# Neighbourhood attention: VectorE takes each lane's maximum right behind its bias, and reciprocals of sums beside the normalising

## The chip, the cores and the metric

The kernel runs on one core of a Trainium2 chip. The time is the device time of one execution in microseconds (us), given as the median of several runs. The core's engines work side by side, each through its own instructions in order: TensorE (PE in the profile), VectorE (DVE), ScalarE (ACT), GpSimd (POOL) and SyncE (SP, which issues the DMAs). They wait for each other by semaphores only.

## The reference, cut to what matters

The program computes a two-layer network with an RWKV mix and a differential attention, and after it a block with two attentions over 512 tokens and a context of 256. The change lies in these two. Each has 8 heads of width 64 for the values. For a head, with 512 + 256 = 768 keys:

```python
# mla: block_attention
sc = einsum('bqhd,bkhd->bhqk', qblk, k) * scale
p = softmax(sc, axis=-1)
o = einsum('bhqk,bkhd->bqhd', p, v)
# na: neighborhood_attention, over a grid of 8 rows by 64 columns
s_win = einsum('bwhd,brwchd->bwhrc', qr, k_win) * scale + bias
s_ctx = einsum('bwhd,blhd->bwhl', qr, kc) * scale
p = softmax(concatenate([s_win, s_ctx], axis=-1), axis=-1)
o = p_win @ v_win + p_ctx @ vc
```

Only the neighbourhood attention adds a bias to its 512 window scores. In the kernel the bias table holds a large negative number outside the window of 16 columns, so all 512 are computed.

## The kernel before, in words

Nearly all of the program is dense layers: pairs of `weights_hi` and `weights_lo` made by ScalarE and VectorE, multiplied on TensorE (line 830). They follow each other with the mixing stages between them, and at the end of every stage each engine waits for the others (`fence`). The two attentions are stages of their own: `attention("mla", ...)` after the layer `uq`, and `attention("na", ...)` after the layers `kb`, `vb` and `qb`.

An attention works on four heads at once. Each has a **lane**, numbered 0 to 3: two PSUM banks (`flat`, 768 scores for 128 queries), a buffer for the probabilities, one for the turned probabilities, and four small columns `attn_small` (maximum, scaled maximum, sum, reciprocal). A head has `TB` = 4 blocks `tb` of 128 queries, each with 5 steps, and `woven` (line 88) writes the order down: step by step, all four lanes at a step before the next. So there are 2 x 4 **rounds**, and in a round every engine goes through its part of steps 0 to 4, lanes 0, 1, 2, 3 at each:

- step 0: TensorE computes the scores (lines 1305 and 1306). It waits for the lane's previous normalising. In `na` VectorE adds the bias (line 2454).
- step 1: VectorE takes the maximum over the 768 scores (line 2462), waits for it, and multiplies it by minus the scale (line 2464). ScalarE computes the exponential with this as its bias, and the sum along with it (line 1777).
- step 2: TensorE transposes the probabilities in six pieces (line 1311). VectorE takes the reciprocal of the sum (line 2468).
- step 3: the turned probabilities are copied out of PSUM, by VectorE in even blocks (line 2471), by ScalarE in odd ones (line 1781).
- step 4: TensorE multiplies by the values (line 1317). VectorE scales the result by the reciprocal (line 2475), which is the normalising.

This one list, `ATTN_ORDER`, sets the order of TensorE, ScalarE and VectorE in both attentions. The plan (`attention_plan`) counts the semaphore values in the same order: each lane has one semaphore for each engine.

The bias tables stand beside it. SyncE loads one for each head (line 2700) into the lane's buffer; for heads 4 to 7 it first waits for the lane's last addition of the head before, lane after lane, and GpSimd adds the window mask to the table (line 2602). VectorE's first addition of a head waits for the mask. Behind these loads SyncE's queue has the next weights.

## Time and profile before

| | us |
|---|---|
| median of 3 runs | 3412.47 |
| lowest and highest of them | 3405.42, 3415.96 |
| the profiled execution's own time | 3388.53 |
| its span, first to last instruction | 3386.7 |
| the mla attention in it, from 2797 to 2911 | 114 |
| the na attention in it, from 3000 to 3137 | 137 |

Times inside the trace are microseconds from the start of the span, and durations in the lists are microseconds unless marked ns. A stretch's clock is the one granted to TensorE, as a share of full speed: 1.00 is 2.4 GHz and 0.50 is 1.2 GHz. In a list in order of time, instructions of one line that follow each other are merged ("x24"), and the brackets give the idle time ahead of them and who ended it.

### The profile page before, as it was taken

The page shows a single profiled execution, that of the slowest core. Times are in us where ns is not written, and L with a number is a line of the kernel's source. Part 1 is how long each engine was busy: PE and PEld are TensorE (multiplying, and loading weights), DVE is VectorE, ACT ScalarE, POOL GpSimd, SP SyncE. Part 2 cuts the span into 40 slices and gives each one's busy share as a digit, 9 for nine tenths or more (in the row PEclk, how much of TensorE's full clock was granted, in tenths as well). Part 3 has the DMA queues.
Part 4 walks back from the last instruction along what each step waited for, and adds up shares of the span by engine and source line. Part 5 has one row for each costly group of instructions (what it writes and reads, how often), then busy time and mean ns, then how long its engine had stood idle before and what let it go on. Part 6 is the DMA issues. An engine that isn't in the chain of part 4 may idle for free.

```text
span 3386.7 us, 39065 instructions
## 1 busy us (share of the span) xinstructions
PE 3149.7 (93%) x15716; PEld 2508.4 (74%) x15716; DVE 1666.8 (49%) x2751; ACT 1149.6 (34%) x1853; POOL 142.1 (4%) x145
## 2 busy tenths in 40 slices
PE   7999889899998889999999999769999989988998
PEld 6888567666667768888788888548888767877886
DVE  5434543456655654344754345775535435245235
ACT  4222133344444333223332224453323333233332
POOL 0000000211211100000000000000000000000000
PEclk9999999799999999999999999779999989987999
DMA  4333232000000033333233332003333110201231
GB/s 127 97 96 94 63 111 75 27 28 28 28 28 15 1 118 100 99 94 100 75 100 94 99 97 88 1 22 101 96 94 95 61 38 1 85 13 47 85 96 56
DMA packets 173896, 234.77 MB, mean 69 GB/s; under 512 B 14201, under 2 KB 111062, under 8 KB 173462
## 3 DMA queue, kind: packets, MB, share of 16 engines
q1 hardware_dynamic: 173718, 232.29, 22.1%
q8 instruction: 125, 2.05, 0.3%
q14 instruction: 53, 0.43, 0.0%
HBM read 228.05 MB, written 4.19 MB: 69 GB/s over the span
## 4 chain that ended last, share of the span: by engine, by line
PE 84%; DVE 9%; ACT 4%; issue 2%; POOL 1%; DMA 0%; SPq 0%; DVEq 0%; ACTq 0%
PE banks L830 63%; PE banks L1317 3%; PE banks L972 2%; PE banks L1311 1%; PE banks L963 1%; PE banks L1305 1%; PE banks L1007 1%; PE banks L1034 1%; PE banks L940 1%; PE banks L1030 1%; PE banks L981 1%; DVE diff_scores L2316 1%; DVE diff_small L2322 1%; PE banks L918 1%; ACT L1556 1%
## 5 line engine op out<-in xcount | busy, mean ns | idle before, releaser
L1865 DVE TENSOR_TENSOR weights_lo<-weights_raw,weights_hi 128x1024 fp32r<-128x1024 f32 (+2 forms) x393 | 472.8, 1206 | 1038.2 <-ACT weights_hi L1388 1036.9
L830 PE MATMUL banks<-operand_hi,weights_hi 128*128 128x512 f32 x2208 | 873.0, 395 | 28.3 <-DVE weights_lo L1865 14.5
L830 PE MATMUL banks<-operand_lo,weights_hi 128*128 128x512 f32 x2208 | 865.9, 392 | 0.0
L830 PE MATMUL banks<-operand_hi,weights_lo 128*128 128x512 f32 x2208 | 865.6, 392 | 0.0
L1388 ACT ACTIVATE weights_hi<-weights_raw 128x1024 fp32r<-128x1024 f32 (+2 forms) x393 | 407.9, 1041 | 1090.9 <-PE banks L830 1049.5
L830 PEld LDWEIGHTS banks<-operand_hi,weights_hi 128*128 128x128 f32 x2208 | 418.4, 189 | 123.2 <-issue 25.8
L830 PEld LDWEIGHTS banks<-operand_lo,weights_hi 128*128 128x128 f32 x2208 | 418.9, 190 | 88.6 <-issue 2.2
L830 PEld LDWEIGHTS banks<-operand_hi,weights_lo 128*128 128x128 f32 x2208 | 418.3, 189 | 88.3
L972 PE MATMUL banks<-operand_lo 128*128 128x512 f32 x370 | 173.2, 492 | 1.3 <-ACT v L1508 1.3
L830 PE MATMUL banks<-hidden_ffn_hi,weights_hi 128*128 128x512 f32 x352 | 137.1, 390 | 0.0
L830 PE MATMUL banks<-hidden_ffn_hi,weights_lo 128*128 128x512 f32 x352 | 136.9, 389 | 0.0
L830 PE MATMUL banks<-hidden_ffn_lo,weights_hi 128*128 128x512 f32 x352 | 136.9, 389 | 0.0
L830 PE MATMUL banks<-hidden_ffn_mid_hi,weights_hi 128*128 128x512 f32 x352 | 136.9, 389 | 0.0
L830 PE MATMUL banks<-hidden_ffn_mid_lo,weights_hi 128*128 128x512 f32 x352 | 136.9, 389 | 0.0
L830 PE MATMUL banks<-hidden_ffn_mid_hi,weights_lo 128*128 128x512 f32 x352 | 136.9, 389 | 0.0
L972 PEld LDWEIGHTS banks<-operand_lo 128*128 128x128 f32 x370 | 70.0, 200 | 27.8 <-issue 22.9
L830 PEld LDWEIGHTS banks<-hidden_ffn_hi,weights_hi 128*128 128x128 f32 x352 | 66.1, 188 | 13.8
L830 PEld LDWEIGHTS banks<-hidden_ffn_mid_hi,weights_hi 128*128 128x128 f32 x352 | 66.1, 188 | 13.8
L830 PEld LDWEIGHTS banks<-hidden_ffn_hi,weights_lo 128*128 128x128 f32 x352 | 66.1, 188 | 13.8
L830 PEld LDWEIGHTS banks<-hidden_ffn_mid_lo,weights_hi 128*128 128x128 f32 x352 | 66.1, 188 | 13.7
L830 PEld LDWEIGHTS banks<-hidden_ffn_mid_hi,weights_lo 128*128 128x128 f32 x352 | 66.1, 188 | 13.7
L830 PEld LDWEIGHTS banks<-hidden_ffn_lo,weights_hi 128*128 128x128 f32 x352 | 66.1, 188 | 13.6
(509 smaller groups left out, 4424.7 us busy)
## 6 DMA issues: line engine op xcount, KB each, us to landing
weights_raw<-in_ffn_w_in_dram SPq DMA_DIRECT2D x352, 256.0 KB, 3.0
weights_raw<-in_ffn_w_out_dram SPq DMA_DIRECT2D x88, 512.0 KB, 3.7
weights_raw<-in_w_in_dram SPq DMA_DIRECT2D x36, 512.0 KB, 3.6
weights_raw<-in_rwkv_w_rkv_dram SPq DMA_DIRECT2D x24, 512.0 KB, 3.8
weights_raw<-in_w_mod_dram SPq DMA_DIRECT2D x24, 512.0 KB, 4.9
weights_raw<-in_w_kv_dram SPq DMA_DIRECT2D x16, 512.0 KB, 3.6
weights_raw<-in_rwkv_w_o_dram SPq DMA_DIRECT2D x8, 512.0 KB, 5.3
weights_raw<-in_diff_w_q_dram SPq DMA_DIRECT2D x8, 512.0 KB, 4.3
```

Of the source, the lines that this page charges most:

```text
L830: mm = nc.tensor.matmul(o, l, r, start=first and t == 0 and job["opens"], stop=last and t == 2, **skip)
L918: mm = nc.tensor.matmul(ps[p0:p0 + c1 - c0, job["bank"]], ring_raw[:, u["ring"], kk, c0:c1], mixed[:, k % 4], start=k == 0, stop=k == KC - 1)
L940: mm = nc.tensor.matmul(ps[0:2, MISC_BANK], sc[:, k], ring_raw[:, units[uid]["ring"], k % 2, :], start=k == 0, stop=k == KC - 1)
L963: mm = nc.tensor.matmul(ps[:, b, tb * 256:(tb + 1) * 256], lhs[h0:h0 + HEAD, tb * P:(tb + 1) * P], L.ar[h0:h0 + HEAD, tb, :, :], start=Tru ...
L972: nc.tensor.matmul(ps[:, IDLE_BANK], two_ident, two_ident.unsqueeze(1).broadcast_to([P, 4, P]), start=True, stop=True)
L981: mm = nc.tensor.matmul(ps[:, b], ring_raw[p0:p0 + n, u["ring"], 0, 0:P], rhs[p0:p0 + n, :], start=j == 0, stop=j == len(ids) - 1)
L1007: mm = nc.tensor.matmul(ps[:, b, p * P:(p + 1) * P], L.mh[:, p], L.inv[:, p], start=True, stop=True)
L1030: mm = nc.tensor.matmul(ps[:, b, p * P:(p + 1) * P], L.xm[:, p], L.inv_t[:, p], start=True, stop=True)
L1034: mm = nc.tensor.matmul(ps[:, b, p * P:(p + 1) * P], L.inv_t[:, p], L.xm[:, p], start=True, stop=True)
L1317: mm = nc.tensor.matmul(ps[:, A, 0:MLA_V], turned_[:, lane, kt * P:(kt + 1) * P], value(hd, kt), start=kt == 0, stop=kt == KEY_TILES - 1)
L1388: nc.scalar.activation(ring_hi[0:p, u["slot"], 0:n, 0:w], ring_raw[0:p, u["ring"], 0:n, 0:w], ACT.Copy).then_inc(*weights_hi.by(i))
L1865: nc.vector.tensor_tensor(ring_lo[0:p, u["slot"], 0:n, 0:w], ring_raw[0:p, u["ring"], 0:n, 0:w], f32(ring_hi[0:p, u["slot"], 0:n, 0:w]), A ...
```

## The change

`ATTN_ORDER` becomes a table with one order for each attention; both are still the same list. VectorE's code changes in two ways. In `na` the maximum and its scaling move from step 1 to step 0, right behind the lane's bias addition, for which the maximum waits. In both attentions the reciprocals move from step 2 to step 4, each ahead of its lane's normalising. The new function `row_maximum` holds the two instructions that `mla` still has in step 1. No instruction is added or taken away.

```diff
--- before.py
+++ after.py
@@ -538,10 +538,10 @@
         operand_plan("cq", 2)
         add_dense("uq", "act", n=4)
         close("uq")
-        ATTN_ORDER = woven(MLA_HEADS, 5 * TB, LANES, False)
+        ATTN_ORDER = {"mla": woven(MLA_HEADS, 5 * TB, LANES, False), "na": woven(NA_HEADS, 5 * TB, LANES, False)}
 
         def attention_plan(name):
-            for hd, lane, s in ATTN_ORDER:
+            for hd, lane, s in ATTN_ORDER[name]:
                 tb, s = divmod(s, 5)
                 if s == 0:
                     lane_pe[lane].expect((name, "s", hd, tb))
@@ -551,15 +551,14 @@
                     lane_dve[lane].expect((name, "max", hd, tb))
                     lane_act[lane].expect((name, "exp", hd, tb))
                 elif s == 2:
-                    lane_dve[lane].expect((name, "rs", hd, tb))
                     lane_pe[lane].expect((name, "turn", hd, tb))
                 elif s == 3:
                     (lane_act if tb % 2 else lane_dve)[lane].expect((name, "turned", hd, tb))
                 else:
                     lane_pe[lane].expect((name, "o", hd, tb))
+                    lane_dve[lane].expect((name, "rs", hd, tb))
                     lane_dve[lane].expect((name, "o", hd, tb))
 
-        attn_lane = {hd: lane for hd, lane, s in ATTN_ORDER}
         attention_plan("mla")
         close("mla")
 
@@ -1292,7 +1291,7 @@
 
             def attention(name, scores, value, prev_ready):
                 probs_, turned_ = probs[name]
-                for hd, lane, s in ATTN_ORDER:
+                for hd, lane, s in ATTN_ORDER[name]:
                     A, B = 2 * lane, 2 * lane + 1
                     flat = ps[:, A:B + 1].rearrange("p a b -> p (a b)")
                     tb, s = divmod(s, 5)
@@ -1768,7 +1767,7 @@
 
             def attention(name, scale):
                 probs_, turned_ = probs[name]
-                for hd, lane, s in ATTN_ORDER:
+                for hd, lane, s in ATTN_ORDER[name]:
                     A, sm = 2 * lane, attn_small[:, lane]
                     flat = ps[:, A:A + 2].rearrange("p a b -> p (a b)")
                     tb, s = divmod(s, 5)
@@ -2440,13 +2439,21 @@
                     dve.wait_ge(*q_sin.at(hd))
                     nc.vector.tensor_tensor(qa[:, hd], qa[:, hd], s, ALU.add).then_inc(*q_done.by(hd))
 
+            def row_maximum(name, hd, lane, tb, scale):
+                sm, flat = attn_small[:, lane], ps[:, 2 * lane:2 * lane + 2].rearrange("p a b -> p (a b)")
+                nc.vector.tensor_reduce(sm[:, 0:1], flat[:, 0:KEYS], AX_X, ALU.max).then_inc(*dve_own.by())
+                dve.wait_ge(*dve_own.now())
+                nc.vector.tensor_scalar(sm[:, 1:2], sm[:, 0:1], -scale, None,
+                                        ALU.mult).then_inc(*lane_dve[lane].by((name, "max", hd, tb)))
+
             def attention(name, o_all, scale):
                 turned_ = probs[name][1]
-                for hd, lane, s in ATTN_ORDER:
+                for hd, lane, s in ATTN_ORDER[name]:
                     A, B, sm, own = 2 * lane, 2 * lane + 1, attn_small[:, lane], lane_dve[lane]
                     flat = ps[:, A:B + 1].rearrange("p a b -> p (a b)")
                     tb, s = divmod(s, 5)
                     if s == 0 and name == "na":
+
                         e0 = NA_KR - 2 - 2 * tb
                         dve.wait_ge(*lane_pe[lane].at((name, "s", hd, tb)))
                         if tb == 0:
@@ -2454,22 +2461,17 @@
                         nc.vector.tensor_tensor(ps[:, A], ps[:, A],
                                                 bias[:, lane, e0:e0 + NA_KR, :].rearrange("p e c -> p (e c)"),
                                                 ALU.add).then_inc(*own.by((name, "bias", hd, tb)))
-                    elif s == 1:
-                        if name == "na":
-                            dve.wait_ge(*own.at((name, "bias", hd, tb)))
-                        else:
-                            dve.wait_ge(*lane_pe[lane].at((name, "s", hd, tb)))
-                        nc.vector.tensor_reduce(sm[:, 0:1], flat[:, 0:KEYS], AX_X, ALU.max).then_inc(*dve_own.by())
-                        dve.wait_ge(*dve_own.now())
-                        nc.vector.tensor_scalar(sm[:, 1:2], sm[:, 0:1], -scale, None,
-                                                ALU.mult).then_inc(*own.by((name, "max", hd, tb)))
-                    elif s == 2:
-                        dve.wait_ge(*lane_act[lane].at((name, "exp", hd, tb)))
-                        nc.vector.reciprocal(sm[:, 3:4], sm[:, 2:3]).then_inc(*own.by((name, "rs", hd, tb)))
+                        dve.wait_ge(*own.at((name, "bias", hd, tb)))
+                        row_maximum(name, hd, lane, tb, scale)
+                    elif s == 1 and name != "na":
+                        dve.wait_ge(*lane_pe[lane].at((name, "s", hd, tb)))
+                        row_maximum(name, hd, lane, tb, scale)
                     elif s == 3 and tb % 2 == 0:
                         dve.wait_ge(*lane_pe[lane].at((name, "turn", hd, tb)))
                         nc.vector.tensor_copy(turned_[:, lane], flat[:, 0:KEYS]).then_inc(*own.by((name, "turned", hd, tb)))
                     elif s == 4:
+                        dve.wait_ge(*lane_act[lane].at((name, "exp", hd, tb)))
+                        nc.vector.reciprocal(sm[:, 3:4], sm[:, 2:3]).then_inc(*own.by((name, "rs", hd, tb)))
                         dve.wait_ge(*lane_pe[lane].at((name, "o", hd, tb)))
                         dve.wait_ge(*own.at((name, "rs", hd, tb)))
                         nc.vector.tensor_scalar(o_all[:, tb, hd * MLA_V:(hd + 1) * MLA_V], ps[:, A, 0:MLA_V], sm[:, 3:4],
```

VectorE's rows around one round of `na`, an even block of the first four heads. `banks` are the scores in PSUM, `lane0_pe` is TensorE's semaphore for lane 0, and so on. Before, steps 0 and 1:

```order
L2454 TENSOR_TENSOR banks<-banks,window_bias 128x512 [waits lane0_pe]
L2454 TENSOR_TENSOR banks<-banks,window_bias 128x512 [waits lane1_pe]
L2454 TENSOR_TENSOR banks<-banks,window_bias 128x512 [waits lane2_pe]
L2454 TENSOR_TENSOR banks<-banks,window_bias 128x512 [waits lane3_pe]
L2462 TENSOR_REDUCE attn_small<-banks 128x1 [waits lane0_dve]
L2464 TENSOR_SCALAR attn_small<-attn_small 128x1 [waits dve_own]
L2462 TENSOR_REDUCE attn_small<-banks 128x1 [waits lane1_dve]
L2464 TENSOR_SCALAR attn_small<-attn_small 128x1 [waits dve_own]
L2462 TENSOR_REDUCE attn_small<-banks 128x1 [waits lane2_dve]
L2464 TENSOR_SCALAR attn_small<-attn_small 128x1 [waits dve_own]
L2462 TENSOR_REDUCE attn_small<-banks 128x1 [waits lane3_dve]
L2464 TENSOR_SCALAR attn_small<-attn_small 128x1 [waits dve_own]
```

Now, the same places:

```order
L2461 TENSOR_TENSOR banks<-banks,window_bias 128x512 [waits lane0_pe]
L2444 TENSOR_REDUCE attn_small<-banks 128x1 [waits lane0_dve]
L2446 TENSOR_SCALAR attn_small<-attn_small 128x1 [waits dve_own]
L2461 TENSOR_TENSOR banks<-banks,window_bias 128x512 [waits lane1_pe]
L2444 TENSOR_REDUCE attn_small<-banks 128x1 [waits lane1_dve]
L2446 TENSOR_SCALAR attn_small<-attn_small 128x1 [waits dve_own]
L2461 TENSOR_TENSOR banks<-banks,window_bias 128x512 [waits lane2_pe]
L2444 TENSOR_REDUCE attn_small<-banks 128x1 [waits lane2_dve]
L2446 TENSOR_SCALAR attn_small<-attn_small 128x1 [waits dve_own]
L2461 TENSOR_TENSOR banks<-banks,window_bias 128x512 [waits lane3_pe]
L2444 TENSOR_REDUCE attn_small<-banks 128x1 [waits lane3_dve]
L2446 TENSOR_SCALAR attn_small<-attn_small 128x1 [waits dve_own]
```

The second lane's addition stood second, ahead of all maxima; now it stands behind the first lane's maximum and scaling.

The rows that follow them in the same round, steps 2 to 4. Before (`na_probs_turned` is the copy of step 3, `na_out` the normalised result):

```order
L2468 RECIPROCAL attn_small<-attn_small 128x1 [waits lane0_act]
L2468 RECIPROCAL attn_small<-attn_small 128x1 [waits lane1_act]
L2468 RECIPROCAL attn_small<-attn_small 128x1 [waits lane2_act]
L2468 RECIPROCAL attn_small<-attn_small 128x1 [waits lane3_act]
L2471 COPY na_probs_turned<-banks 128x768 [waits lane0_pe]
L2471 COPY na_probs_turned<-banks 128x768 [waits lane1_pe]
L2471 COPY na_probs_turned<-banks 128x768 [waits lane2_pe]
L2471 COPY na_probs_turned<-banks 128x768 [waits lane3_pe]
L2475 TENSOR_SCALAR na_out<-banks,attn_small 128x64 [waits lane0_dve,lane0_pe]
L2475 TENSOR_SCALAR na_out<-banks,attn_small 128x64 [waits lane1_dve,lane1_pe]
L2475 TENSOR_SCALAR na_out<-banks,attn_small 128x64 [waits lane2_dve,lane2_pe]
L2475 TENSOR_SCALAR na_out<-banks,attn_small 128x64 [waits lane3_dve,lane3_pe]
```

Now:

```order
L2471 COPY na_probs_turned<-banks 128x768 [waits lane0_pe]
L2471 COPY na_probs_turned<-banks 128x768 [waits lane1_pe]
L2471 COPY na_probs_turned<-banks 128x768 [waits lane2_pe]
L2471 COPY na_probs_turned<-banks 128x768 [waits lane3_pe]
L2474 RECIPROCAL attn_small<-attn_small 128x1 [waits lane0_act]
L2477 TENSOR_SCALAR na_out<-banks,attn_small 128x64 [waits lane0_dve,lane0_pe]
L2474 RECIPROCAL attn_small<-attn_small 128x1 [waits lane1_act]
L2477 TENSOR_SCALAR na_out<-banks,attn_small 128x64 [waits lane1_dve,lane1_pe]
L2474 RECIPROCAL attn_small<-attn_small 128x1 [waits lane2_act]
L2477 TENSOR_SCALAR na_out<-banks,attn_small 128x64 [waits lane2_dve,lane2_pe]
L2474 RECIPROCAL attn_small<-attn_small 128x1 [waits lane3_act]
L2477 TENSOR_SCALAR na_out<-banks,attn_small 128x64 [waits lane3_dve,lane3_pe]
```

The four reciprocals stood between the last scaling and the first copy. Now nothing stands there, and each reciprocal is directly ahead of its lane's normalising. In `mla` the reciprocals move in the same way, and in odd blocks there are no copies on VectorE.

## Rows read from the trace of the kernel before

**Rows 1.** The page, parts 1 and 2: busy us, share, instructions; slices

```profile
PE 3149.7 (93%) x15716; PEld 2508.4 (74%) x15716; DVE 1666.8 (49%) x2751; ACT 1149.6 (34%) x1853; POOL 142.1 (4%) x145
...
PEclk9999999799999999999999999779999989987999
```

**Rows 2.** Stage table: length, PE, PEld, DVE, ACT, POOL busy, clock, DMA; mla, then na

```profile
2797.00:2911.00 114.00, 110.41 (x704) 88.83 (x704) 60.88 (x144) 44.03 (x81) 0.00 (x0) 0.98 0.00 1
3000.00:3137.00 137.00, 109.81 (x704) 100.00 (x704) 78.53 (x175) 43.56 (x81) 8.24 (x4) 0.80 0.10 29
```

**Rows 3.** Waits of the na stage (3000 to 3138): total, times, longest us

```profile
PE banks L1311 <- ACT na_probs L1777: 27.0, 8, 3.5
```

**Rows 4.** Chain of waits, one na round: start us, us, what

```profile
3034.72 1.06 PE banks L1305 x4
3035.78 0.43 PE banks L1306 x3
...
3036.24 2.59 DVE banks L2454 x4
3038.83 0.86 DVE attn_small L2462
...
3039.72 0.17 DVE attn_small L2464
...
3039.90 1.00 ACT na_probs L1777 x2
...
3040.95 5.38 PE banks L1311 x24
3046.33 5.47 PE banks L1317 x48
```

**Rows 5.** Stage table by stretches of this round, columns as in rows 2

```profile
3040.00:3046.00 6.00, 5.05 (x24) 5.05 (x25) 5.03 (x13) 3.87 (x8) 0.00 (x0) 0.50 0.00 1
3046.00:3047.00 1.00, 1.00 (x9) 1.00 (x7) 1.00 (x2) 0.00 (x0) 0.00 (x0) 0.72 0.07 16
3047.00:3052.00 5.00, 5.00 (x46) 4.93 (x46) 1.71 (x5) 0.00 (x0) 0.00 (x0) 1.00 0.00 0
```

**Rows 6.** TensorE in order of time, this round: start us, us, instructions, idle before

```profile
3036.90 0.70 PE L1306 MATMUL banks<-na_keys,na_queries 64*128 64x256 f32 x4
3040.95 5.38 PE L1311 MATMUL banks<-ident,na_probs 128*128 128x128 f32 x24 [3.35 <-ACT na_probs L1777]
```

**Rows 7.** TensorE in order of time, mla stage, an even block

```profile
2859.85 2.13 PE L1311 MATMUL banks<-ident,mla_probs 128*128 128x128 f32 x18
```

**Rows 8.** VectorE in order of time, the same na round

```profile
3038.74 0.95 DVE L2462 TENSOR_REDUCE attn_small<-banks 128x1 f32<-128x768 f32 x1
...
3039.79 0.95 DVE L2462 TENSOR_REDUCE attn_small<-banks 128x1 f32<-128x768 f32 x1
...
3042.87 0.15 DVE L2464 TENSOR_SCALAR attn_small<-attn_small 128x1 f32<-128x1 f32 x1
...
3049.16 0.28 DVE L2475 TENSOR_SCALAR na_out<-banks,attn_small 128x64 f32<-128x64 f32 x1 [1.06 <-PE banks L1317]
```

**Rows 9.** ScalarE in order of time, na, an odd block: copies of the turned

```profile
3061.04 2.20 ACT L1781 ACTIVATE na_probs_turned<-banks 128x768 f32<-128x768 f32 x3
```

**Rows 10.** One line and one tile: count, min/median/max ns: additions, reciprocals

```profile
L2454 DVE TENSOR_TENSOR banks<-banks,window_bias x32: 689/690/700, 3002.0 to 3123.5; 128x512 f32<-128x512 f32 x32
...
L2468 DVE RECIPROCAL attn_small<-attn_small x64: 142/149/166, 2805.4 to 3129.5; 128x1 f32<-128x1 f32 x64
```

**Rows 11.** Chain of waits, mla stage, an even block

```profile
2862.25 0.17 DVE attn_small L2468
2862.42 0.86 DVE mla_probs_turned L2471
```

**Rows 12.** Waits of the mla stage (2797 to 2911)

```profile
PE banks L1317 <- DVE mla_probs_turned L2471: 0.7, 4, 0.2
```

**Rows 13.** GpSimd in order of time, na stage: the masks of the later heads

```profile
3061.06 6.16 POOL L2602 TENSOR_TENSOR window_bias<-window_bias,window_mask 128x896 f32<-128x896 f32 x3 [0.46 <-DMA window_bias<-in_rpb_dram]
```

## The prediction

> **What bounds the kernel now.** I read the page first: TensorE is busy 93% of the span, VectorE 49%, and TensorE's clock falls from full in only a few slices [rows 1]. So a change on VectorE counts only where TensorE stands waiting for it. The change touches two stages, and the stage table shows how different they are. The latent attention ("mla", 114 us) keeps TensorE busy for 110.41 us at a granted clock of 0.98. The neighbourhood attention ("na", 137 us) has it busy for 109.81 us at a clock of 0.80 [rows 2]. The waits of the second stage say for what: TensorE waits 27.0 us, in 8 waits, for ScalarE's exponential [rows 3]; the chain below leads on to VectorE. There are 8 because the stage has 8 rounds (2 groups of 4 heads by 4 query blocks).
>
> The chain of waits through one round tells what VectorE has on the path [rows 4]: scores 1.49 us, all four bias additions 2.59, one maximum 0.86 and its scaling 0.17, one exponential 1.00, then TensorE's 24 transposes 5.38 and the 48 passes with the values 5.47. With the gaps that is 17.1 us, and 8 rounds are the stage. The other three maxima are not on the path. They run beside the transposes. The granted clock of this round is 0.50 from 3040 to 3046 and 1.00 from 3047 [rows 5]. That is 1.2 GHz for the transposes, after TensorE stood idle for 3.35 us [rows 6]. One transpose costs 5.38/24 = 0.224 us there, and 2.13/18 = 0.118 us in the mla stage at full clock [rows 6, 7].
>
> **The order of VectorE in na.** Before, in the round at 3036.24: four additions, then four pairs of maximum and scaling. The first scaling starts at 3039.72, the fourth at 3042.87, so they follow each other at 1.05 us; ScalarE starts lane 0's exponential 0.18 us after its scaling, at 3039.90 [rows 4, 8]. Now the maximum waits for the addition just issued. An addition takes 0.70 us (689 to 700 ns, [rows 10]) while four of them in a row took 2.59 [rows 4], so (2.59 - 0.69)/3 = 0.63 us each when nothing waits. The price of a dependent pair I take from maximum to scaling, 3038.74 to 3039.72: 0.98 us from start to start for an instruction of 0.95 [rows 4, 8], so 0.03 behind the end. So lane 0's maximum starts at 3036.24 + 0.73 = 3036.97, its scaling 0.98 later at 3037.95, that is **1.77 us earlier**. Each next lane needs 0.73 + 0.98 + 0.07 (3039.72 to 3039.79, scaling to the next start [rows 4, 8]) = 1.78 us instead of 1.05: scalings at 3039.73, 3041.51, 3043.29. Lane 3 is **0.42 us later** than before. The exponentials follow, and TensorE can transpose lane 3 from 3043.29 + 0.18 + 1.05 = 3044.52 (1.05: exponential start 3039.90 to transpose start 3040.95 [rows 4]).
>
> **What TensorE makes of it.** It starts lane 0 at 3040.95 - 1.77 = 3039.18. At 1.2 GHz a lane's six transposes take 1.35 us, so it is through with lane 2 before lane 3 is ready, stands about 0.4 us between lanes, and ends at 3044.52 + 1.35 = 3045.87 instead of 3046.33 (3040.95 + 5.38). The gain is 0.46 us a round, not 1.77: what is late next is the last lane's maximum. The value passes can follow at once, in even blocks because VectorE copies lane 0 from 3043.36, in odd ones because ScalarE does from about 3044.5 at 0.73 each (2.20/3, [rows 9]). But the clock rose only behind the transposes: the microsecond from 3046 is at 0.72, so 0.56 of it was low and the rise came at 3046.56 [rows 5]. If it stays there, 0.46 us more of value passes run at 1.2 GHz and 0.22 us of the gain goes back (0.46 x (1 - 0.118/0.224), the passes taken as slowing like the transposes). That leaves 0.24 us a round, 8 x 0.24 = **1.9 us**. Bounds for this term: 8 x 0.46 = 3.7 us if the rise comes earlier by as much; a loss if it comes later (second rival).
>
> The self-wait was priced at 0.73 - 0.63 = 0.10 us a lane, 0.4 us a round. The additions show what a missing wait is worth: they follow each other at 0.63 us though each lasts 0.69. The Trainium skill ("VectorE: DVE Perf Modes", The DRAIN you can't avoid) reports eight copies that took the same time with and without a semaphore behind each, and takes such a semaphore to cost nothing. By that rule the last lane would be level with before, each round about 0.4 us shorter, and the sum some 3 us better. The trace's additions don't agree with it, so I keep my price.
>
> **The reciprocals.** 64 of them, 142 to 166 ns [rows 10], move behind the copies and stand before the normalising of their lane. In the mla stage the one of lane 3 holds back lane 0's copy in even blocks: 0.17 us in the chain, then the copy 0.86, and TensorE waits 0.18 us for it; 4 waits, 0.7 us [rows 11, 12]. Without it the copy starts right behind the last scaling, beside lane 3's exponential of 1.00 us, and is done before TensorE needs it: **0.7 us** saved. In na the transposes hide it. In the new place they are free: VectorE idles 1.06 us before each normalising [rows 8], the sum is long there, and the next scores wait only for lane 0's normalising, three lanes earlier. The cover holds as long as a lane's passes (5.47/4 = 1.37 us) exceed 0.28 + 0.15.
>
> **What moves with it.** SyncE reloads a lane's bias table only after that lane's last addition. In round 4 these now come at steps of 1.78 us instead of 0.63, the last 3 x 1.15 = 3.4 us later. GpSimd's last mask then ends near 3067.2 + 3.4 = 3070.6 [rows 13]; VectorE's addition for that lane comes in round 5, two rounds after this one, at 3036.24 + 2 x 17.1 + 3 x 1.78 = 3075.8. Hidden, with 5 us to spare; so are the weight loads behind it in SyncE's queue, needed after the stage's end at 3137. TensorE's and ScalarE's own orders are unchanged.
>
> **Sum.** 1.9 + 0.7 = 2.6 us: 3388.53 of the profiled execution becomes 3385.9. That execution lies 0.7% below the median of the three timed runs, 3412.47, which themselves spread over 10.5 us. I set the sum against the median: **3410 us**, 0.08% less. What a measurement of this kernel can tell from no change is about 0.3%, 10 us; the gain is far under it.
>
> **Rivals.** (1) *The clock no longer falls.* TensorE now idles only from 3037.6 (3036.90 + 0.70, [rows 6]) to 3039.18, 1.6 us instead of 3.35, and mla's shorter waits left its clock at 0.98. Then lane 3 ends at 3044.52 + 0.71 = 3045.23, 1.10 us a round: 8.8 + 0.7 = 9.5 us, 3403. Against it: until 3044.5 TensorE would work 0.71 us in each 1.78. (2) *The clock rises later: slower.* It rose 5.6 us after TensorE had begun to work without a gap (3040.95 to 3046.56). Now the work is unbroken only from 3044.52. If the rise follows that start as before, it comes at 3050.1, and 4.2 us of value passes run at 1.2 GHz where 0.2 did: 4.0 x 0.47 = 1.9 us back, 1.9 - 0.46 = +1.4 a round, some +11.5 in 8, less 0.7 is 3423. The gain of 0.46 is used up when 1.0 us more of the passes is low, that is by a rise at about 3047.1. I hold it second, because at the low clock TensorE would still be busy for 1.35 of each 1.78 us, and only the last gap of 0.4 lies near the rise. The Trainium skill ("TensorE: Matmul & The Clock Gate", A second HAM failure mode) describes a kernel in which short idle stretches between groups of matmuls kept the clock going down and up. By that rule this rival comes first and the time is 3423; no stretch of this trace shows such gaps inside a burst of transposes. (3) *The order is neutral*: the rise moves so that each round takes 17.1 us as before, since VectorE's work in a round is the same; with mla's 0.7 that is 3412. The rows of the changed order leave no doubt that it does what it says.
>
> **How the numbers follow.** Forecast (within a few us of 3410) 0.60; first rival 0.06; second 0.26, of which about half lies beyond the 10 us; neutral 0.08. Range: from the first rival, 3402, to the second, 3424. Faster by over 0.3%: 0.06, the first rival with a little help; slower: 0.15; within: 0.79.
>
> **What would show it.** Right: in na, additions and maxima alternate, scalings 1.78 us apart; TensorE's first wait near 1.6 us and three of about 0.4; clock 0.50 through the transposes; rounds of 16.8 to 17.1 us; mla rounds of even blocks 0.18 shorter. Wrong: value passes for microseconds at 0.50 (rounds over 17.5 us), or no fall of the clock (rounds of 16.0).

## The result and the profile after

The changed kernel takes 3410.79 us (median of 20 runs, 3403.64 to 3440.4), the kernel before 3397.97 us in as many (3382.91 to 3421.27). The ratio is **1.0042**, 95% interval 1.0021 to 1.0062: slower by 0.4%. The forecast was 3410 us, 0.08% less, too little to tell from no change. Its 3410 us lies beside the measured median only because the three runs of before that it started from, 3412.47 us, stood above the median that more runs gave. That is luck. The ratio is what counts, and it went the other way.

The profiled executions are 3388.53 us before and 3407.91 us now. The difference is 19.4 us. One place is 20.9 us longer, the na stage (136.7 us from its first to its last matmul before, 157.6 now); mla gave back 1.6.

The stage table of the changed kernel, mla and na, columns as in [rows 2]:

```profile
2797.00:2910.00 113.00, 109.53 (x704) 88.78 (x704) 61.25 (x145) 44.08 (x81) 0.00 (x0) 0.98 0.00 1
3001.00:3159.00 158.00, 128.29 (x704) 107.84 (x704) 81.25 (x176) 42.95 (x80) 8.24 (x4) 0.75 0.09 26
```

In mla TensorE is busy for nearly the same time (109.53 us, before 110.41) at the same clock. In na its 704 matmuls are the same ones, but they cost 128.29 us instead of 109.81, at a granted clock of 0.75 instead of 0.80. So TensorE waited only 2.5 us longer (29.7 us not busy against 27.2); it worked more slowly. The waits of the na stage, beside [rows 3]:

```profile
ACT na_probs L1776 <- DVE attn_small L2446: 110.8, 32, 16.5
...
PE banks L1310 <- ACT na_probs L1776: 29.6, 32, 1.9
```

29.6 us in 32 waits, where it was 27.0 in 8: the one wait of 3.35 us in each round has become four short ones.

The chain of waits through na, all of its eight value passes (start us, us, what); one round before had 5.47 [rows 4]:

```profile
3013.08 10.13 PE banks L1316 x48
...
3035.30 5.40 PE banks L1316 x48
...
3052.09 10.13 PE banks L1316 x48
...
3074.90 5.42 PE banks L1316 x48
...
3091.77 10.13 PE banks L1316 x48
...
3113.99 5.40 PE banks L1316 x48
...
3130.78 10.13 PE banks L1316 x48
...
3153.50 5.40 PE banks L1316 x48
```

Here is the time. In the first, third, fifth and seventh round the passes take 10.13 us, in the others 5.40. Rounds are 22.1, 17.5, 21.5, 18.1, 21.6, 17.5, 21.5 and 17.8 us long, where all were about 17.1.

TensorE in order of time, the third round, beside [rows 6]:

```profile
3042.89 0.70 PE L1305 MATMUL banks<-na_keys,na_queries 64*128 64x256 f32 x4
3045.18 0.88 PE L1310 MATMUL banks<-ident,na_probs 128*128 128x128 f32 x6 [1.59 <-ACT na_probs L1776]
3046.97 0.87 PE L1310 MATMUL banks<-ident,na_probs 128*128 128x128 f32 x6 [0.91 <-ACT na_probs L1776]
3048.76 1.54 PE L1310 MATMUL banks<-ident,na_probs 128*128 128x128 f32 x6 [0.91 <-ACT na_probs L1776]
3050.55 1.54 PE L1310 MATMUL banks<-ident,na_probs 128*128 128x128 f32 x6 [0.25 <-ACT na_probs L1776]
3051.88 10.34 PE L1316 MATMUL banks<-na_values,na_probs_turned 128*128 128x64 f32 x48
3062.15 2.08 PE L1304 MATMUL banks<-na_keys,na_queries 64*128 64x512 f32 x4
```

The wait ahead of lane 0 is 1.59 us, and there is a gap ahead of every lane. Two lanes are transposed at full clock (0.87 us), then the clock falls and two take 1.54; the 48 passes of 64 columns follow without any gap for 10.34 us, and the next scores take 2.08 us instead of 1.14. By stretches, beside [rows 5]:

```profile
3044.00:3048.00 4.00, 1.75 (x12) 1.27 (x12) 3.86 (x8) 2.27 (x5) 0.00 (x0) 0.97 0.00 0
3048.00:3052.00 4.00, 3.00 (x14) 2.60 (x14) 3.93 (x6) 1.70 (x4) 0.00 (x0) 0.50 0.02 6
3052.00:3062.00 10.00, 10.00 (x49) 10.00 (x48) 2.15 (x9) 0.00 (x0) 0.00 (x0) 0.50 0.00 0
3062.00:3065.00 3.00, 3.00 (x12) 1.73 (x13) 0.28 (x1) 0.00 (x0) 0.00 (x0) 0.53 0.00 0
3065.00:3071.00 6.00, 3.15 (x21) 2.00 (x19) 5.76 (x10) 2.46 (x5) 0.96 (x1) 1.00 0.63 160
```

TensorE was busy for all of the 10 us from 3052 and stayed at 0.50, that is 1.2 GHz. It came back to 1.00 only within the next scores, which are 512 and 256 columns wide: the stretch from 3062 is at 0.53, that from 3065 at 1.00.

The fourth round begins its last two lanes with the same gaps, to 0.01 us, and also at the low clock:

```profile
3071.57 1.53 PE L1310 MATMUL banks<-ident,na_probs 128*128 128x128 f32 x6 [0.91 <-ACT na_probs L1776]
3073.36 1.54 PE L1310 MATMUL banks<-ident,na_probs 128*128 128x128 f32 x6 [0.26 <-ACT na_probs L1776]
```

Yet its passes take 5.42 us: the clock is 0.50 until 3075 and 0.99 in the microsecond behind it. So the gaps make a bad round possible, but they don't decide alone which round is bad.

VectorE in order of time, the same round, beside [rows 8]:

```profile
3042.22 0.70 DVE L2461 TENSOR_TENSOR banks<-banks,window_bias 128x512 f32<-128x512 f32 x1 [1.20 <-PE banks L1305]
3042.96 0.96 DVE L2444 TENSOR_REDUCE attn_small<-banks 128x1 f32<-128x768 f32 x1
3043.95 0.15 DVE L2446 TENSOR_SCALAR attn_small<-attn_small 128x1 f32<-128x1 f32 x1
3044.02 0.69 DVE L2461 TENSOR_TENSOR banks<-banks,window_bias 128x512 f32<-128x512 f32 x1
...
3045.74 0.15 DVE L2446 TENSOR_SCALAR attn_small<-attn_small 128x1 f32<-128x1 f32 x1
...
3049.31 0.15 DVE L2446 TENSOR_SCALAR attn_small<-attn_small 128x1 f32<-128x1 f32 x1
```

This is as forecast: scalings 1.78 to 1.79 us apart, the maximum 0.74 us behind the start of its addition (forecast 0.73).

### The profile page after: what moved, and what is told of

It reads as the page before. It is cut to its first block, busy times and chain, and to the rows that moved or that the text cites. A ratio compares the mean times of both kernels' runs of the same rounds, so it can differ in the third digit from the quotient of the medians.

```text
span 3406.1 us, 39065 instructions
## 1 busy us (share of the span) xinstructions
PE 3164.3 (93%) x15716; PEld 2514.8 (74%) x15716; DVE 1670.3 (49%) x2751; ACT 1149.2 (34%) x1853; POOL 141.6 (4%) x145
## 4 chain that ended last, share of the span: by engine, by line
PE 83%; DVE 10%; ACT 4%; issue 2%; POOL 1%; DMA 0%; SPq 0%; DVEq 0%; ACTq 0%
PE banks L829 63%; PE banks L1316 3%; PE banks L971 2%; PE banks L1304 1%; PE banks L962 1%; DVE attn_small L2444 1%; PE banks L1006 1%; PE banks L1033 1%; PE banks L939 1%; PE banks L1029 1%; PE banks L980 1%; DVE diff_scores L2315 1%; DVE diff_small L2321 1%; PE banks L917 1%; DVE banks L2461 1%
## 5 line engine op out<-in xcount | busy, mean ns | idle before, releaser
L829 PE MATMUL banks<-hidden_ffn_hi,weights_lo 128*128 128x512 f32 x352 | 136.9, 389 | 0.0
L829 PE MATMUL banks<-hidden_ffn_lo,weights_hi 128*128 128x512 f32 x352 | 136.9, 389 | 0.0
L829 PE MATMUL banks<-hidden_ffn_mid_hi,weights_hi 128*128 128x512 f32 x352 | 136.9, 389 | 0.0
L829 PE MATMUL banks<-hidden_ffn_mid_lo,weights_hi 128*128 128x512 f32 x352 | 136.9, 389 | 0.0
L829 PE MATMUL banks<-hidden_ffn_mid_hi,weights_lo 128*128 128x512 f32 x352 | 136.9, 389 | 0.0
L971 PEld LDWEIGHTS banks<-operand_lo 128*128 128x128 f32 x370 | 70.0, 200 | 27.8 <-issue 22.9
```

Of the source, the lines that this page charges most:

```text
L829: mm = nc.tensor.matmul(o, l, r, start=first and t == 0 and job["opens"], stop=last and t == 2, **skip)
L971: nc.tensor.matmul(ps[:, IDLE_BANK], two_ident, two_ident.unsqueeze(1).broadcast_to([P, 4, P]), start=True, stop=True)
```

## The experiments

Two theories stood against each other. **The clock**: the gaps between the lanes' transposes let it fall and keep it from rising behind them, and the narrow value passes cannot bring it back. **The order**: VectorE's new order costs the time itself, by its self-waits, by the later last lane, or by the reciprocals in front of the normalising. "na" is the stage from its first to its last matmul in the profiled execution of each kernel; 136.7 us before, 157.6 changed. Ratios are against the kernel before on the same chip. Each of them has its own group of runs, and a single profiled execution need not be the median one.

**One half at a time.** First the reciprocals alone, on the kernel before:

```diff
-                    elif s == 2:
-                        dve.wait_ge(*lane_act[lane].at((name, "exp", hd, tb)))
-                        nc.vector.reciprocal(sm[:, 3:4], sm[:, 2:3]).then_inc(*own.by((name, "rs", hd, tb)))
                     elif s == 4:
+                        dve.wait_ge(*lane_act[lane].at((name, "exp", hd, tb)))
+                        nc.vector.reciprocal(sm[:, 3:4], sm[:, 2:3]).then_inc(*own.by((name, "rs", hd, tb)))
                         dve.wait_ge(*lane_pe[lane].at((name, "o", hd, tb)))
```

> The kernel before with the reciprocals moved beside the normalising, in both attentions; the maxima stay where they were. Clock theory (the time went into TensorE's clock, because the maxima behind their biases tear gaps into the transposes): nothing of the loss is here. The na stage stays at 136.7 us with rounds of 17.1 us and the clock at 0.50 only for the transposes; mla shortens from 113.2 to 111.6 us as in the changed kernel; in all 1 to 2 us less than before, no change that can be measured. Rival (the reciprocal in front of each normalising holds up TensorE's next scores): na grows towards 157 us and the time by 10 us or more.

Measured: ratio 0.9987 (0.9957 to 1.0016), na 136.9 us, seven of the eight rounds between 16.9 and 17.2, mla 111.4 instead of 113.2. None of the loss is here.

Then the maxima alone: the changed kernel with the two reciprocal lines put back into step 2.

> The changed kernel with the reciprocals put back behind the exponentials: only the maxima are moved. Clock theory: the whole loss is here. The na stage takes about 157 us, with rounds of some 21.5 us in which the 48 value passes take 10.1 us at 1.2 GHz and rounds of 17.5 us between them; mla is at 113 us as before; the time is 0.4 to 0.6% over before. Rival (reciprocals): na at 137 us.

Measured: ratio 1.0052 (1.0021 to 1.0084), na 153.8 us, mla 113.2. The value passes on its chain of waits, in the order of the rounds:

```profile
3014.47 10.13 PE banks L1316 x48
...
3036.69 5.40 PE banks L1316 x48
...
3053.47 10.13 PE banks L1316 x48
...
3075.44 5.40 PE banks L1316 x48
...
3091.79 9.31 PE banks L1316 x48
```

The passes of the other three rounds take 5.40, 9.24 and 5.41 us, so four of eight are long again. The loss is in the maxima: 17.1 of the 20.9 us of the na stage in this execution, and a timed ratio no smaller than the changed kernel's.

The fifth round shows something more. All four lanes are transposed at full clock (0.87 to 0.88 us each, with gaps of 0.93 to 0.94 us between them), the passes begin at full clock, and it falls about 1.3 us into them: the microsecond from 3092 is at 1.00, that from 3093 at 0.56, and the rest at 0.50. So the transposes need not run slowly for the passes to.

**The order kept, the gaps closed.** The changed kernel, with one wait more on TensorE:

```diff
                     elif s == 2:
+                        if name == "na" and lane == 0:
+                            pe.wait_ge(*lane_act[1].at((name, "exp", hd + 1, tb)))
                         pe.wait_ge(*lane_act[lane].at((name, "exp", hd, tb)))
```

> The changed kernel with one wait more: in na TensorE starts lane 0's transposes only when lane 1's exponential is done too. VectorE's order is that of the changed kernel. Clock theory: at 1.2 GHz the transposes then run from 4.7 us behind the first bias addition without a gap (1.35 us for a lane, the lanes come at 1.78), the clock rises behind them as before, the value passes are at full clock, rounds are 17.1 us and na takes 137 to 138 us; the time is level with before. Rival (the loss is VectorE's order: self-waits, the last lane's maximum 0.42 us later, work held up on its queue): a wait added can give nothing back, na stays at 157 us or more.

Measured: ratio 0.9979 (0.9950 to 1.0009), na 136.9 us, rounds of 17.1. TensorE in order of time:

```profile
3039.16 5.38 PE L1312 MATMUL banks<-ident,na_probs 128*128 128x128 f32 x24 [3.39 <-ACT na_probs L1778]
3044.34 5.65 PE L1318 MATMUL banks<-na_values,na_probs_turned 128*128 128x64 f32 x48
```

24 transposes in one piece, 3.39 us of idle time ahead of them, the same 5.38 us as in [rows 6], and passes at 5.65. A wait **added** takes back the 20 us, with VectorE's order untouched. It does two things at once: it closes the gaps between the lanes, and it gathers the idle time in one stretch ahead of them. No run here does one without the other.

**The other way round: the old order, with gaps.** Into the kernel before go unread additions that space the maxima like the new order does, and the same wait on TensorE closes the gaps again in a second kernel:

```diff
                         nc.vector.tensor_scalar(sm[:, 1:2], sm[:, 0:1], -scale, None,
                                                 ALU.mult).then_inc(*own.by((name, "max", hd, tb)))
+                        if name == "na" and lane < LANES - 1:
+                            nc.vector.tensor_tensor(sq_sum[:, :], rstd[:, :], rstd[:, :], ALU.add)
```

> The kernel before, in its old order; only, behind the scalings of lanes 0, 1 and 2 in na VectorE makes one addition of 128x512 in SBUF that nobody reads (about 0.65 us), so that the scalings come at 1.7 us instead of 1.05 and the transposes get the gaps of the changed kernel. By VectorE's work alone lane 3 comes about 2.0 us later, its transposes end 1.2 us later and rounds take 18.3 us: na 146 us. Clock theory: in every second round or more the value passes run at 1.2 GHz as well (10.1 us), such rounds take about 23 us, and na is 160 us or more, although the order of the change is not there. Rival (the loss comes with the new order): 146 us.

> The kernel with the spaced maxima, and TensorE starts lane 0's transposes only when lane 1's exponential is done too. VectorE's work is the same, the gaps in the transposes are gone. Clock theory: value passes are at full clock in most rounds, which take 18.2 to 19 us; na is 146 to 152 us, less than without the wait. Rival: the same as without the wait, or more.

Measured: 1.0047 (1.0013 to 1.0081) with na 157.4 us, and 1.0002 (0.9971 to 1.0033) with na 154.5. The first is the loss in the old order, though under the 160 us expected: only two of eight rounds have long passes (10.13 and 10.15 us), not every second one, and one of the two is the round spoken of below. In the second one round of 25.6 us was left, against the expectation. VectorE in that round:

```profile
3059.34 0.68 DVE L2469 TENSOR_TENSOR squares_sum<-rstd 128x512 f32<-128x512 f32 x1
...
3060.99 2.57 DVE L2469 TENSOR_TENSOR squares_sum<-rstd 128x512 f32<-128x512 f32 x1
...
3064.54 1.51 DVE L2469 TENSOR_TENSOR squares_sum<-rstd 128x512 f32<-128x512 f32 x1
```

The addition in SBUF takes 0.68 us elsewhere, but 2.57 and 1.51 beside GpSimd's masks, which ran from 3060.94. The experiment had torn gaps of its own (TensorE waited 0.72 and 0.95 us inside the transposes). So the pair was repeated without the additions in that one round:

```diff
-                        if name == "na" and lane < LANES - 1:
+                        if name == "na" and lane < LANES - 1 and (hd >= LANES or tb < TB - 1):
```

> The kernel with the spaced maxima again, but without the unread additions in the one round in which GpSimd adds its masks (there they had taken up to 2.6 us beside GpSimd, and torn gaps of their own). By VectorE's work alone na takes 7 rounds of 18 and one of 17.1 us: 144 us. Clock theory: one round or more still has its value passes at 1.2 GHz (10.1 us), na over 150 us.

> The same with TensorE's wait for lane 1's exponential ahead of lane 0's transposes: no gaps in any round now. Clock theory: no round has its value passes at 1.2 GHz; rounds of 17.5 to 19 us, na 142 to 146 us, and less than without the wait. Rival (the first round of the other pair, in which the wait did not help, was not GpSimd's doing): a round of over 20 us again.

Measured: without the wait 1.0057 (1.0023 to 1.0092), na 160.3 us, three rounds of 22.5 to 22.9 and one of 20.4; with it 1.0019 (0.9987 to 1.0052), na **144.3** us, no round over 19.0. The order is the old one in both and VectorE's work is the same; closing the gaps is worth 16 us. The medians of the timed runs, on one chip, are as far apart: 3415.62 and 3399.42 us.

Over all these kernels the count is plain. In 40 rounds the clock fell and the transposes then ran in one piece (before, the reciprocals alone, the wait added to the changed kernel, and the spaced kernels where the gaps were closed or left out); their passes took at most 5.7 us in every one. In 40 rounds there were gaps between the lanes (changed, the maxima alone, the spaced ones, and the changed kernel with five unread matmuls a round below); in 16 of them the passes took 9.2 us or more, in the others at most 5.6.

**TensorE kept busy.** If its own idling makes the clock fall, unread matmuls should hold it up. They go into the quarter of lane 3's second bank that holds no scores, and lane 3's maximum waits for them:

```diff
                     elif s == 2:
+                        if name == "na" and lane in {0: 12}:
+                            spare = ps[:, 2 * LANES - 1, CTX:T]
+                            for _ in range({0: 12}[lane]):
+                                mm = nc.tensor.matmul(spare, ident[:, :], f32(op[0][:, 0, 0:T - CTX]), start=True, stop=True)
+                            if lane == 0:
+                                mm.then_inc(*filler.by((hd - lane, tb)))
                         pe.wait_ge(*lane_act[lane].at((name, "exp", hd, tb)))
```

> The kernel before; in na TensorE makes 12 matmuls of 128x256 that nobody reads while it waits for lane 0's exponential (into an unused quarter of lane 3's bank, and lane 3's maximum waits for them). Clock theory: TensorE is no longer idle for 3.35 us a round, so the clock stays at 1.00; transposes cost 0.12 us instead of 0.22, but lane 3's wait for its exponential (44.1 on the clock of the round shown) now ends last: rounds of about 15.8 us, na 126 to 128 us, the time 9 to 11 us (0.3%) under before. Rival (the granted clock has a cause other than TensorE's own idling here, or the filler lands on the path): na stays at 137 us or grows.

Measured: 0.9986 (0.9959 to 1.0012), na 136.1 us at a clock of 1.00. The clock part was right and the time (126 to 128 us expected) was not: the 12 took 5.45 us in a wait of 3.35, since each is two passes of 0.227, so the filler itself came onto the path. With 7 of them, and with the reciprocals moved or not:

> The kernel before with the reciprocals moved and 7 unread matmuls of 128x256 ahead of lane 0's transposes (3.2 us; with 12 they took 5.45 us and held up lane 3's maximum and the transposes). Clock theory: clock 1.00 through na, transposes 0.12 us each, lane 3's end 10.1 us behind the start of the scores, rounds 15.5 us, na 125 us instead of 136.9; mla 111.6 us; 12 to 14 us (0.4%) under before. If the filler still lands on the path, rounds stay over 16.5 us.

> The kernel before with the 7 unread matmuls alone, reciprocals where they were. Clock theory: as the kernel with the reciprocals moved, but lane 3's reciprocal holds up the first copy in even blocks now that the transposes no longer hide it: rounds of 15.9 us in even blocks and 15.5 in odd ones, na 126 us, mla 113 us; 10 us (0.3%) under before. Rival: no change from before.

Measured: with the reciprocals moved 0.9954 (0.9922 to 0.9985), na **125.0** us, rounds of 15.5 to 15.7; without, 0.9977 (0.9944 to 1.0009), which is not clear of no change, na 126.8 us, rounds of 16.0 and 15.7 in turn. TensorE in order of time, the first of these two:

```profile
3036.70 3.29 PE L1313 MATMUL banks<-operand_hi,ident 128*128 128x256 f32 x14
3040.12 0.87 PE L1318 MATMUL banks<-ident,na_probs 128*128 128x128 f32 x6
3041.17 0.88 PE L1318 MATMUL banks<-ident,na_probs 128*128 128x128 f32 x6 [0.18 <-ACT na_probs L1784]
...
3043.30 0.88 PE L1318 MATMUL banks<-ident,na_probs 128*128 128x128 f32 x6 [0.20 <-ACT na_probs L1784]
```

Six transposes take 0.87 us, and the waits of 0.2 us between lanes do no harm, since the clock is up and stays up. With the reciprocals moved this is the one kernel whose interval lies under 1. Its mla stage took 113.0 us and not the 111.6 expected: from 2799 to 2808 us, at its first scores, the clock was 0.59 in this execution.

The same on the changed kernel (`{0: 3, 1: 2}`, the last one signalling), where only two of the four gaps can be filled, since lane 3's maximum then reads the bank:

> The changed kernel; in na TensorE makes 3 matmuls of 128x256 that nobody reads ahead of lane 0's transposes and 2 ahead of lane 1's (0.45 us each, into the unused quarter of lane 3's bank, whose maximum waits for them). Its gaps ahead of lanes 2 and 3 stay. Clock theory: the clock stays at 1.00 or falls in few rounds; where it stays, lane 3's transposes end about 10.5 us behind the start of the scores and rounds take 15.9 us, na 128 us or, with some rounds low, up to 145; in no case 157. The cost of VectorE's order without the clock is then the difference to the next kernels: some 0.3 us a round. Rival (VectorE's order costs the 20 us): na stays at 157 us.

Measured: na 141.9 us; six rounds have passes of 5.3 to 5.4 us, two of 10.13. The rounds entirely at full clock take 16.1 us, against 15.6 to 15.7 with the old order: that 0.4 to 0.5 us a round, some 3.6 us in all, is what the order itself costs. The timed runs do not show this gain over the changed kernel: 1.0036 (1.0001 to 1.0070). Two gaps left open, of 0.91 to 0.93 us, are enough for the clock to fall in some rounds, and how many it is in the other executions stays open.

**Wide matmuls ahead of the narrow ones.** Why does the clock stay low through 10 us of unbroken work? The changed kernel with five wide unread matmuls right ahead of the value passes:

```diff
                         pe.wait_ge(*(lane_act if tb % 2 else lane_dve)[lane].at((name, "turned", hd, tb)))
+                        if name == "na" and lane == 0:
+                            for _ in range(5):
+                                nc.tensor.matmul(ps[:, B, CTX:T], ident[:, :], f32(op[0][:, 0, 0:T - CTX]), start=True, stop=True)
```

> The changed kernel; in na TensorE makes 5 unread matmuls of 128x256 right ahead of lane 0's value passes (2.3 us in all at 2.4 GHz, 4.3 at 1.2). In the changed kernel's bad rounds the 48 value passes of 64 columns follow each other for 10.1 us without a gap and the clock stays at 1.2 GHz until the next scores, which are 512 wide. If it is their narrowness that keeps it there, the wide ones bring the clock up within the round: no round has all passes at 1.2 GHz, the passes take 8 us or less in the bad rounds, and the next scores are at full clock. Rival (the clock comes back only so long after the gaps, whatever TensorE does): passes of 10.1 us at 1.2 GHz as before, na 157 us plus 8 x 2.3 to 4.3.

Measured: na 153.8 us, less than the changed kernel's 157.6 although 8 x 2.3 us of work at the least was added; over all runs 1.0081 (1.0046 to 1.0116). The chain of waits, two of the rounds whose transposes fell to 1.2 GHz, the wide ones (L1317) and the passes (L1319):

```profile
3012.99 4.03 PE banks L1317 x10
3017.02 5.30 PE banks L1319 x48
...
3051.98 3.32 PE banks L1317 x10
3055.30 5.30 PE banks L1319 x48
```

The passes of all eight rounds take 5.30 to 5.32 us. The wide matmuls begin at 1.2 GHz and take 4.03 or 3.32 us instead of 2.25, and behind them the clock is up. The expectation held in full in this execution. So the clock does not simply come back a fixed time after the gaps: in the changed kernel the passes at this place left it low. Whether it is the 64 columns of a pass or something else in which the two kinds of matmul differ was not tried. The kernel is no improvement in itself, since the wide ones cost about what they save.

## Why the prediction was wrong

**The loss came by the second rival** ("the clock rises later: slower"), which had 0.26. It had the kind of loss right, passes at 1.2 GHz behind a late rise. It was held second for a wrong reason, was sized at half, and its rule for the rise, 5.6 us after the last gap, held in none of the changed kernel's eight rounds.

**The step that failed** is "If it stays there", the assumption under *What TensorE makes of it* that the rise comes at the same place as before, just behind the transposes. The changed kernel's chain shows that in four of eight rounds it does not come there at all. The fall was misplaced too. The sum lets all 24 transposes run at 1.2 GHz (1.35 us a lane), as before. In no round of the changed kernel did they: in the second and sixth none fell to it, in the first three lanes, in the others about two. What spoke against the rival, TensorE busy for 1.35 of each 1.78 us at the low clock, was no reason: all three other kernels with such gaps (the maxima alone moved, and the two spaced ones) have rounds in which the passes run at the low clock, and with the gaps closed by a wait it rose, but for the one round in which VectorE's unread additions, beside GpSimd's masks, made new ones.

**The size.** The rival lets the rise come 5.6 us after the last gap, so that 4 us of passes run low: +1.4 us a round, 11.5 in all. Measured are 20.9. In the third round the rise came about 14 us after the last gap (3050.55), in the fourth, with the same gaps, 1.6 us after it (3073.36). The rival took it for granted that any unbroken work brings the clock up. The value passes don't: in a bad round all 48 are low (10.13 - 5.40 = 4.7 us more), and the first of the next scores with them (2.08 us against 1.14). Four rounds are 4.4 to 4.8 us longer than their counterparts before, 18.2 us; the other four, which begin with scores at the low clock, 0.4 to 1.0 us, 2.7 in all. These are no worse because behind the scores the clock is back at 1.00. In the second and sixth round it stays there, in the fourth and eighth it falls and returns as the passes begin. So bad and good rounds alternate, which the forecast, with eight equal rounds, did not see. Why the fourth and eighth get the clock back in time and the third and seventh don't stays open.

**VectorE's terms** were right, or nearly. Scalings come 1.78 us apart (sum: 1.78), lane 0's is 1.75 us earlier behind the first addition (sum: 1.77), and the fourth starts 7.09 us behind it, before 6.63: 0.46 later (sum: 0.42). The first wait was put at 1.6 us and is 1.59. The self-wait was priced at 0.10 us. The maximum starts 0.74 us behind its addition. In the kernel before a maximum whose own addition was long done starts 0.60 us behind the last addition (3038.74 in [rows 8], less 3036.24 + 2.59 - 0.69 in [rows 4]), so the wait costs 0.14 us a lane, and the price, taken from additions at 0.63 us, was a little low. So the rule of the Trainium skill ("VectorE: DVE Perf Modes", The DRAIN you can't avoid), by which the semaphore costs nothing, does not hold for this pair, and the round at full clock with its 0.4 to 0.5 us says the same.

**The reciprocals** were right in sign and small in size: 0.7 us forecast, 1.6 measured in mla (113.2 to 111.6), and 1.8 with the reciprocals alone. The chain of waits there, changed kernel, beside [rows 11]:

```profile
2862.34 0.87 PE banks L1310 x6
2863.21 0.84 PE banks L1316 x8
```

The reciprocal and the copy are gone from it; TensorE goes from its transposes straight into the passes, which also take 5.31 us in even blocks instead of 5.57. The forecast had only the wait. What the 0.26 us of the passes come from was not tried. In na they cost and gain nothing while the clock falls ("the transposes hide it"); at full clock, beside the unread matmuls, they are worth 0.44 us in an even block (rounds of 16.03 against 15.59).

**The bias tables** stayed hidden, as forecast: GpSimd's masks ended at 3078.28 and no wait for them is in the list of waits.

**The first rival** (the clock no longer falls, 0.06) was rightly small: in the profiled execution it fell six times in eight rounds. The rule of the Trainium skill that would have put the second rival first ("TensorE: Matmul & The Clock Gate", A second HAM failure mode: short idle stretches between groups of matmuls keep the clock going down and up) agrees with the trace, in which the clock goes down and up and rounds take about 22 and 18 us in turn. The forecast set it aside because no stretch of the old trace showed such gaps. That is the error to learn from, for the change itself was about to make them: its own sum had 0.4 us between lanes.

## What to carry to other kernels

Where TensorE runs at its low clock, ask what brings it up again, and whether the change touches that: up to 5.4 us of transposes without a gap did it in every round here, and gaps of 0.25 to 0.9 us between the lanes undid it in four rounds of eight. Handing work over earlier is no gain if it arrives in pieces; a wait of TensorE until its work comes in one block was worth 20 us in na. Better still is to fill its idle time, where a bank is free for it: seven unread matmuls a round, with the reciprocals moved, took na from 137 to 125 us.

## What the runs showed of the hardware

Unbroken work did not always bring the clock up. Behind 48 fp32 passes of 64 columns, 10.1 us without a gap at 0.211 us each, it was still at 1.2 GHz in each of the changed kernel's bad rounds. Behind the scores, behind the unread 128x256 matmuls and, within 0.7 us at most, behind the transposes in one piece it was at 2.4. In two rounds of the kernel with only the maxima moved it even fell while the passes ran without a gap. The kernel before could not show this, since its clock rose about 0.2 us after its passes began.

Three kernels begin na differently and settle at the same round: before 17.31 us, then 17.07 to 17.11; with the reciprocals moved 17.41, then 17.07 to 17.15; with the wait added 17.52, then 17.06 to 17.12. Each has the clock at 0.50 once a round, for the transposes. What draws them to that length was not tried.

An addition in SBUF on VectorE took up to 2.57 us instead of 0.68 beside GpSimd's masks, while the bias additions in PSUM, in the changed kernel, kept their 0.69 beside them (at 3070.41).

Executions of one kernel differ by about 1% (before: 3383 to 3421 us). In three of the profiled executions the mla stage begins at 2820 to 2824 us instead of 2795 to 2801; at least part of the time goes into the RWKV stage, where from 800 to 1217 us the granted clock is 0.94 in the kernel before and 0.89 in the one with 12 unread matmuls:

```profile
800.00:1217.00 417.00, 365.21 (x2766) 280.11 (x2767) 245.58 (x553) 172.14 (x328) 75.77 (x78) 0.94 0.08 29
```

The same table of the kernel with 12 unread matmuls:

```profile
800.00:1217.00 417.00, 376.22 (x2704) 290.29 (x2703) 233.48 (x531) 161.03 (x311) 75.73 (x78) 0.89 0.05 15
```

No kernel changes anything there. For differences of half a per cent, the stage in the profile told more than the totals, as long as it is remembered that it is one execution.
